# A hybrid decoder step on one Trainium2 core: how the routed token rows are stored and gathered, and throwaway products while TensorE waits for the routing

## The reference

```python
m = mixer(rmsnorm(h, g_mix), ...)          # one input projection, short conv + retention, w_o
h = h + m
# routing and experts, on x = rmsnorm(h, g_ffn)
g_prob = softmax(x @ w_rg + b_rg);  g_top, g_idx = top_k(g_prob, 1)       # 4 groups
e_sel  = (x @ w_re + b_re) of the chosen group                            # 8 experts in it
e_top, e_idx = top_k(softmax(e_sel), 2)
for e in range(32):
    y = y + cw[:, e:e+1] * ((silu(x @ w_gate[e]) * (x @ w_up[e])) @ w_down[e])
h = h + y
h = h + (p @ w_ple_proj) * sigmoid(rmsnorm(h, g_ple) @ w_ple_gate)
y_out = rmsnorm(h, g_final)
```

## Time and profile before

| | us |
|---|---|
| median of 3 runs | 858.21 (857.88 to 858.45) |
| the profiled execution's own time | 857.27 |
| its span in the trace | 855.4 |
| TensorE busy | 713.4 (83%) |
| mean DMA rate over the span | 301 GB/s |

### The profile page before, as it was taken

One profiled execution on the slowest core, in us unless ns is written; L12 is line 12 of the kernel. 1 busy time (PEld: TensorE's weight loads), 2 busy tenths in 40 slices (PEclk: granted clock), 3 DMA queues, 4 the chain that ended last, 5 costly groups with the idle time before them and its releaser, 6 DMA issues.

```text
span 855.4 us, 10929 instructions
## 1 busy us (share of the span) xinstructions
PE 713.4 (83%) x4302; PEld 434.9 (51%) x4302; DVE 279.8 (33%) x498; ACT 181.7 (21%) x275; POOL 104.2 (12%) x163
## 2 busy tenths in 40 slices
PE   5999999999999389888777777777777777778995
PEld 5998899989998133332222222222222222223685
DVE  6464578575433621110100101101001001015774
ACT  6242312223323100100000000000000000006666
POOL 0500000000010312112111121121111111100000
PEclk9999999999999599999999999999999999999898
DMA  9541216542845877999999999999999999993201
GB/s 363 200 174 52 73 62 228 215 178 75 343 139 190 289 300 332 378 428 425 426 427 427 428 426 425 429 424 428 426 428 427 428 423 428 425 415 143 99 27 74
DMA packets 32865, 257.18 MB, mean 301 GB/s; under 512 B 6468, under 2 KB 7028, under 8 KB 19128
## 3 DMA queue, kind: packets, MB, share of 16 engines
q1 hardware_dynamic: 24944, 237.17, 67.5%
q0 software_dynamic: 7024, 18.07, 5.6%
q10 hardware_dynamic: 864, 1.48, 0.5%
HBM read 249.96 MB, written 15.13 MB: 310 GB/s over the span
## 4 chain that ended last, share of the span: by engine, by line
PE 47%; DMA 39%; DVE 3%; issue 2%; ACT 1%; SPq 1%; POOL 0%; DVEq 0%; POOLq 0%
DMA arena<-in_w_exp 38%; PE ps L1496 19%; PE ps L1671 12%; PE ps L1794 4%; PE ps L1686 3%; PE ps L1529 2%; PE ps L1600 1%; PE ps L1623 1%; DMA h_rows<-xh 1%; PE ps L1590 1%; SPq L528 1%; PE ps L1504 1%; PE ps L1770 1%; DVE region_u L1316 0%; ACT region_u L818 0%
## 5 line engine op out<-in xcount | busy, mean ns | idle before, releaser
L1671 PE MATMUL ps<-arena,region_u 128*64 128x512 f32 x992 | 227.5, 603 | 58.0 <-DMA arena<-in_w_exp 57.1
L1671 PEld LDWEIGHTS ps<-arena,region_u 128*64 128x64 f32 x992 | 70.3, 138 | 213.6 <-issue 139.0
L1316 DVE SCALAR_TENSOR_TENSOR region_u<-ps,small,region_u 128x256 f32<-128x256 f32 x32 | 15.5, 484 | 392.1 <-ACT region_u L818 392.1
L1496 PE MATMUL ps<-u_hi,w_hi 128*128 128x260 f32 x448 | 130.0, 290 | 11.3 <-DVE w_low L1099 8.6
L1496 PE MATMUL ps<-u_lo,w_hi 128*128 128x260 f32 x448 | 127.6, 285 | 0.0
L1496 PE MATMUL ps<-u_hi,w_low 128*128 128x260 f32 x448 | 127.3, 284 | 0.0
L1686 PE MATMUL ps<-arena,region_u 128*64 128x512 f32 x496 | 113.3, 598 | 7.8 <-DMA arena<-in_w_exp 3.7
L1496 PEld LDWEIGHTS ps<-u_hi,w_hi 128*128 128x128 f32 x448 | 85.4, 191 | 12.6 <-issue 12.3
L1496 PEld LDWEIGHTS ps<-u_hi,w_low 128*128 128x128 f32 x448 | 85.4, 191 | 0.0
L1496 PEld LDWEIGHTS ps<-u_lo,w_hi 128*128 128x128 f32 x448 | 85.3, 190 | 0.2
L651 POOL DMA_INDIRECT y_rows<-region_v,scol x32 | 33.3, 1041 | 377.4 <-ACT region_v L822 377.4
(11 more groups left out here) (270 smaller groups left out, 796.7 us busy)
## 6 DMA issues: line engine op xcount, KB each, us to landing
arena<-in_w_exp SPq DMA_DIRECT2D x91, 2048.0 KB, 25.8
arena<-in_w_in SPq DMA_DIRECT2D x36, 512.0 KB, 3.3
arena<-in_w_exp SPq DMA_DIRECT2D x8, 512.0 KB, 4.0
arena<-in_w_ple_gate SPq DMA_DIRECT2D x2, 2048.0 KB, 23.6
region_q<-in_w_exp SPq DMA_DIRECT2D x12, 256.0 KB, 12.6
region_q<-in_xt SPq DMA_DIRECT2D x4, 520.0 KB, 6.5
region_u<-in_xt SPq DMA_DIRECT2D x2, 1040.0 KB, 5.9
arena<-in_state_ret POOLq DMA_DIRECT2D x2, 1024.0 KB, 8.7
```

What stands on the lines that cost most here:

```text
L1316: V.scalar_tensor_tensor(hs[b], ps[:, 2 + b, 256:512], rs[b], sg[b], ALU.mult, ALU.mult).then_inc(out_sem, 1)
L1496: last = mm(halves(out)[:, half, :], w[:, k, :], u[:, cols], start=(k == 0 and s == 0), stop=(k == KD - 1 and s == 2))
L1671: last = mm(ps[side * 64:side * 64 + 64, 2 + b, :], xv[:, k // 4, k % 4, :], rows(k % 4 * 2 + side), start=(k == 0), stop=(k == KD - 1))
```

## The change

Four edits. (1) GpSimd stores all four steps of token rows, without the 1/rms columns between them. (2) The 1/rms columns are written to memory by ScalarE (before: VectorE, inside the routing) and stored by four DMAs on ScalarE's queue under a semaphore of their own, `rstd_stored`; the gather now waits for `h_stored`, `rstd_stored` and `index_done`. (3) SyncE waits for `h_stored` before it asks for spare unit 1 (four pieces), and for the first gather before it asks for any of spare unit 2 (eight pieces; before, three of them were asked for ahead of the gather). (4) TensorE does products of the identity with itself, whose results nobody reads: 44 calls in job `rk` before the wait for `chosen_done`, 16 in job `ix` before the wait for `hot_done`, 28 at the end of job `tot`, before the first `rows_t`.

```diff
+SPIN = (44, 16, 28)
@@ SyncE
             load_first(5)
             load_spare(0, 4)
+
+            sp.wait_ge(h_stored, 16 * 2 * len(STORES))
             for n in range(4):
                 load_spare(1, n)
-            for n in range(3):
-                load_spare(2, n)
             sp.wait_ge(xg_loaded[0], 16)
-            for n in range(3, 8):
+            for n in range(8):
                 load_spare(2, n)
@@ GpSimd
-            for c0, c1 in STORES[:-1]:
+            for c0, c1 in STORES:
                 store_rows(c0, c1)
-
-            pool.wait_ge(rows_ready, 1)
-            for half in range(2):
-                pool.dma_start(h_full[:, :, half, 512:HR], rstd_rows[:, 0:4, :]).then_inc(h_stored, 16)
-                pool.dma_start(h_few[:, half, 512:HR], rstd_rows[0:NB, 4, :]).then_inc(h_stored, 16)
-            store_rows(*STORES[-1])
...
-            pool.wait_ge(h_stored, 16 * (2 * len(STORES) + 4))
+            pool.wait_ge(h_stored, 16 * 2 * len(STORES))
+            pool.wait_ge(rstd_stored, 16 * 4)
             pool.wait_ge(index_done, 1)
@@ ScalarE, behind the last tp
+            act.wait_ge(rstd_done, 2)
+            act.wait_ge(pe_jobs, HEAD.pe(("wo", KD - 1)))
+            nc.scalar.activation(rstd_rows, stats[:, 10:15].unsqueeze(2).to_broadcast([P, NT, HR - 512]),
+                                 ACT.Copy).then_inc(rows_ready, 1)
+            act.wait_ge(rows_ready, 1)
+            for half in range(2):
+                act.dma_start(h_full[:, :, half, 512:HR], rstd_rows[:, 0:4, :]).then_inc(rstd_stored, 16)
+                act.dma_start(h_few[:, half, 512:HR], rstd_rows[0:NB, 4, :]).then_inc(rstd_stored, 16)
@@ VectorE, between route_logits() and route_choose()
-                        V.tensor_copy(rstd_rows, wide(stats[:, 10:15], [P, NT, HR - 512])).then_inc(rows_ready, 1)
@@ TensorE
+            def spin(out, count):
+
+                for _ in range(count):
+                    mm(out[:, 0:P], ident[:, :], ident[:, :], start=True, stop=True)
...
                 elif kind == "rk":
 
+                    spin(b, SPIN[0])
                     pe.wait_ge(lt_loaded, 16)
                     pe.wait_ge(chosen_done, 1)
...
                 elif kind == "ix":
 
+                    spin(b, SPIN[1])
                     pe.wait_ge(hot_done, 1)
...
                 elif kind == "tot":
                     for s in range(NT):
                         last = mm(b[:, 0:NE], lt16[:, 1, :], chosen[:, s, :], start=(s == 0), stop=(s == NT - 1))
+                    spin(pair(n + 1), SPIN[2])
```

More of the change, by code:

```diff
@@ L366, in build @@
         h_stored, lt_loaded, rows_ready = sem("h_stored"), sem("lt_loaded"), sem("rows_ready")
+        rstd_stored = sem("rstd_stored")
         pp_loaded = sem("pp_loaded")
```

## The result

The changed kernel takes 859.68 (median of 20; 858.53 to 860.93), the kernel before 857.79 in the same set (20; 856.36 to 858.98). The ratio is 1.0027 with a 95% interval of 1.0021 to 1.0033: 0.27% slower, about 2 (1.89 between the medians). The forecast was 861.9 in a range of 858.0 to 864.5, with 0.69 on slower. The profiled execution has a span of 857.9.

What follows compares the result with a forecast made beforehand. The end of the first `gate_up` was taken to move `gu_done` 4, the weight stream and the end one to one. +7.2 at `rows_t`, -0.5 transposes, -2.96 `gate_up` gave +3.7; 858.21 + 3.7 = 861.9, range 858.0 to 864.5.

Steps and rivals of the forecast that it cites:

- No effect: Rival: the expert stage takes the delay up and the time stays at 858; chance 0.04.
- The price of a call: TensorE's identity products: each call costs two records, 0.2225 at full clock.
- The rival of cheap products: Rival: a TensorE identity product costs 0.111, the products fit into the waits, 852.8; chance 0.13.
- The steps at full clock: TensorE: `rk` 0.4, blocks 9.79, 3.56 and 6.23, transposes save 0.5, first `gate_up` saves 2.96.
- Block C: The 28 calls ending job `tot`: 6.23 long, ending at 299.4, 2.7 behind the gathered data.
- I take 4.5, and 3.5 to 5.6 as bounds: TensorE's time at low clock from the first block on, half the work done meanwhile, adding 4.5/2.
- block A: The 44 calls in job `rk`: 9.79 at full clock, 12.0 with the low clock, ending at 288.4.
- the rival at 0.15 with +1.5: Rival: TensorE's clock does not fall at 276, all is 2.25 sooner, +1.5, 859.7; chance 0.15.
- the likeliest case: The whole delay: products outlast their gaps, +3.7, 861.9, spanning 860.9 to 863.0; chance 0.58.
- This edit alone is worth between 0.9 and 2.2: Edits 1 and 2: the earlier stores stop holding back the gather, a gain of 0.9 to 2.2.
- the bound of 287.9 for the landing of the 1/rms columns: ScalarE's queue: issues end by 280.6, and the slowest store's 7.30 behind that gives 287.9 at the latest.
- Price nothing: Edit 3: the moved spare units cost 0; a late piece would cost below 4.9.

Runs made afterwards that it cites:

- e7: The changed kernel with 24, 9 and 20 calls of products and both spare units asked for after the first gather: 852.76, ratio 0.9943.
- e3: The kernel before with the three blocks of products (44, 16, 28 calls) and nothing else of the change: 860.78, ratio 1.0037.
- e10: The changed kernel with every block of products doubled to 88, 32 and 56 calls: 879.56, ratio 1.0254.
- e6: The changed kernel without products, both spare units asked for only after the first gather: 855.60, ratio 0.9977.
- e2: The changed kernel with half the products, 22, 8 and 14 calls: 858.92, ratio 1.0013.
- e9: The changed kernel with 24, 9 and 20 calls of products, loads as in the change: 857.71, ratio 0.9992.
- e1: The changed kernel with the three blocks of products empty, stores and spare units as in the change: 858.03, ratio 1.0007.
- e11: The changed kernel without products, spare units as before the change, 1/rms columns stored on GpSimd's queue behind the token rows: 857.70, ratio 1.0001.
- e5: The changed kernel without products, spare units as before the change, 1/rms columns on ScalarE's queue: 860.48, ratio 1.0043.
- e12: The changed kernel with its 44, 16 and 28 calls, both spare units asked for after the first gather: 860.12, ratio 1.0024.
- e8: The kernel before with 24, 9 and 20 calls of products and nothing else of the change: 855.18, ratio 0.9975.
- e4: The changed kernel with 44, 16 and 28 transposes of the identity in place of products: 858.67, ratio 1.0012.

## Why the prediction was right, point by point

*The bound.* One to one from the first `gate_up` to `gu_done` 4, 2.82 and 2.82, and nearly so to the end, with a span 2.4 longer. All the profiles bear it out: in 13 of the 14 the span ends 550.6 to 551.5 behind the end of the first `gate_up`, which itself lies anywhere from 299.2 (e7) to 307.7 (e3); in e10 it ends 549.8 behind. Shown again by e10's time, where 19.6 asked for gave 19.9. "No effect" is out.

*The price of a call.* 0.2225 from the earlier trace rows was forecast and 0.2234 measured. The rival of cheap products is out. The Trainium skill, page "TensorE: Matmul & The Clock Gate", section "Why this matters for your kernels", says to leave no long idle gaps between bursts of matmuls. The runs agree where the filler fits its gap: e7 takes 2.8 off e6. Where it does not fit, the cost is larger than the gain: in the changed kernel the first `gate_up` did run at full clock and 2.74 was had, but `rows_t` came 5.37 later for it.

*The size.* The delay was forecast as 3.7 and measured as 1.9, so only the range, which also reached down to no effect, held the time. Of the 2.2 between 861.9 and 859.68, 0.4 is the base (858.21 from three runs, 857.79 from twenty) and 1.8 the delay. By the prediction's own band for no change, 856.5 to 859.9, the result would even count as none; twenty executions of each kernel tell it from zero. What was too large is below.

*The steps at full clock.* `rk` 0.37 (0.4), the blocks 9.83, 3.67 and 6.35 (9.79, 3.56, 6.23), `rows_t` to `gate_up` -0.65 (-0.5), `gate_up` -2.74 (-2.96). One step was left out: from the end of the index (291.99) to the gather (293.06) GpSimd needs 1.07, where the sum had 0.05. Block C ends 2 behind the data, so it did no harm.

*The time at low clock: mis-sized.* "I take 4.5, and 3.5 to 5.6 as bounds" failed. Where the clock falls at 276 it is back 2.4 after the block begins (e3) and block A is 11.04, not 12.0: it costs 1.2 and not 2.25. The three rows that I read all count from the start of a dense stretch that begins 3 or more after the fall, or at the start of the kernel; here the fall lies just ahead of it. And in the profiled execution of the changed kernel it did not fall at 276 at all, which was the rival at 0.15 with +1.5; from the transposes on it measured +1.98, but it had paid for a fall at 251. The 20 executions are not all alike either: 11 have a mean granted clock of 0.990 (median 859.9) and 9 one of 0.992 or more (859.2). Which stretch ran faster in these nine isn't shown, as only one execution was profiled. All that the change touches comes after 272, where SyncE's order first differs, so it can't have caused the fall at 251. Over the 14 profiles of this case the clock fell at about 251 in three (the changed kernel, e2, e9), between 274.7 and 277.7 in nine, at 280.4 in e1 and not before the gather in e8. What decides it from one execution to the next stays open. So the sign, the mechanism and the place were right and the range held the time, but the likeliest case's own range, 860.9 to 863.0, did not. The step that failed in it is the term of 4.5 at low clock.

*The stores.* "This edit alone is worth between 0.9 and 2.2": wrong. With the spare units as before it is worth nothing with the 1/rms columns on GpSimd's queue (e11) and costs 2.6 by the medians, 3.7 by the ratio, with them on ScalarE's (e5). Two steps failed. The 2.2 at best left out GpSimd's 1.07 from the index to the gather; in e1, where no store holds the gather, it goes 1.2 earlier. And the bound of 287.9 for the landing of the 1/rms columns was too early: it took the slowest store of GpSimd's for ScalarE's, which landed at 291.3. I looked at the issue alone. The Trainium skill, page "Trainium Kernel Development and Optimization", section "Key Constraints", says that DMAs from the several queues run on the same 16 DMA engines and interleave, and that another queue saves only issue time. The trace agrees that a queue of its own gives no shelter from the loads (11.86), but here the queue also changed the landing itself, which was 8.01 on GpSimd's (e11).

*The spare units.* "Price nothing" is true of the change (e12) and untrue of the stage. I looked at whether the third expert gets its weights in time, which it does, and not at what the moved 2 MB run beside: e1 loses 2.1 by them, and e9 against e7 loses 4 to 5, as the idle time that they make also drops the clock in most executions. The edits 1 to 3 together gain nothing (e1), and with one line moved gain 2.3 (e6).

## What to carry to other kernels

A filler on an in-order engine is free only up to the end of the gap: multiply the calls by a measured price (here two records a call) and lay it against the gap, since gaps of 0.9 (e2) and 0.6 (e8) left over still kept the clock, while blocks 6 longer than their gaps held the work behind them back by 5.4. When a load is moved behind an event, ask what else that event releases: the landing of the stores released both the 2 MB and the gather that they were to make room for. And take the queue and the traffic beside it into the landing time of a small store, for the issue says little (the size of the pieces may be part of it; that was not tried alone).

## What the runs showed of the hardware

The fall of TensorE's clock behind light work is not tied to a place in the program. Executions of kernels with the same head had it at 250.8 (changed kernel), 275.7 (e3) or 280.4 (e1), and where dense work went on the clock was back 3.4 later (changed kernel, e3). So one profile's clock row is one draw: 12 executions of the same kernel e9 spread from 854.6 to 860.2, in step with their mean granted clock. A block of 44 fp32 transposes that began at low clock had the full clock 2.2 after its start (e4), as the block of products did (2.4, e3).
